# Nine pages of a first projection multiplied in high and low halves, with a norm and a clearing moved, in a two-block kernel on one Trainium2 core

## What is computed

```
h = rms_norm(x, norm1_g)
proj = h @ w_in
p_rwkv, p_sb, q_mem, gate_logits = split(proj)
y_a = rwkv7_branch(p_rwkv)          # token shift, low-rank paths, recurrence over 8 heads of 64
y_b = stick_breaking_branch(p_sb)   # q, k, v of 512 columns each
y_m = memory_branch(q_mem, mem)     # mem normed with mem_norm_g, then projected
x   = x + (sum of gated branches) @ w_out
x   = x + conv_ffn(x)
```

## Time and profile before

| | |
|---|---|
| runs | 1413.20, 1414.07, 1414.85 us |
| profiled execution, its span | 1414.9 us |
| PE busy | 1281.9 us (91%) |
| DVE, ACT, POOL busy | 835.0, 626.0, 585.6 us |
| chain that ended last | PE 59%, DMA 28%, DVE 6%, ACT 5% |
| mean granted TensorE clock | 0.988 |

### The profile page before, as it was taken

How to read it: one execution, slowest core, us unless ns; L and a number is a source line. 1 busy time by engine, 2 the same in 40 slices (tenths; PEclk the granted TensorE clock), 3 DMA queues, 4 the chain that set the end, 5 groups by cost and what they waited for, 6 DMA issues and landing times.

```text
span 1414.9 us, 22174 instructions
## 1 busy us (share of the span) xinstructions
PE 1281.9 (91%) x8684; PEld 904.4 (64%) x8684; DVE 835.0 (59%) x1897; ACT 626.0 (44%) x1449; POOL 585.6 (41%) x390
## 2 busy tenths in 40 slices
PE   7999999999999999999999999999778878777786
PEld 5887897888999999987897544444222323222222
DVE  3865210445557873477347676667776666677744
ACT  3310232556566665553454444444443444444433
POOL 1100022414878888740043544444434443343341
PEclk9999999999999999999999999999999999999999
DMA  6332321333545556542368999999999999999995
GB/s 240 105 120 92 105 93 60 120 105 134 195 164 186 181 186 194 165 134 98 137 232 340 421 421 421 422 421 422 421 422 421 421 418 422 422 422 422 422 422 226
DMA packets 67652, 381.06 MB, mean 269 GB/s; under 512 B 7520, under 2 KB 7648, under 8 KB 34528
## 3 DMA queue, kind: packets, MB, share of 16 engines
q0 software_dynamic: 36864, 268.45, 45.7%
q1 hardware_dynamic: 29808, 107.49, 22.5%
q10 hardware_dynamic: 880, 3.76, 0.7%
HBM read 378.63 MB, written 1.05 MB: 268 GB/s over the span
## 4 chain that ended last, share of the span: by engine, by line
PE 59%; DMA 28%; DVE 6%; ACT 5%; issue 2%; POOL 1%; DVEq 0%; POOLq 0%; ACTq 0%
DMA arena_block<-in_experts,arena_block 26%; PE bank L429 24%; PE bank L1023 10%; PE bank L465 4%; PE bank L983 3%; PE bank L483 3%; DVE arena_block L2218 2%; PE bank L427 2%; PE bank L447 2%; PE bank L853 1%; PE bank L516 1%; ACT arena_block L1517 1%; PE bank L542 1%; ACT arena_block L1515 1%; POOL w_lo L2276 1%
## 5 line engine op out<-in xcount | busy, mean ns | idle before, releaser
L1023 PE MATMUL bank<-arena_block 128*128 128x512 f32 x1024 | 494.8, 618 | 102.3 <-ACT arena_block L1517 102.3
L1023 PEld LDWEIGHTS bank<-arena_block 128*128 128x128 f32 x1024 | 183.1, 192 | 402.0 <-ACT arena_block L1517 246.0
L2218 DVE SCALAR_TENSOR_TENSOR arena_block<-arena_block 128x1024 f32<-128x1024 f32 x256 | 313.6, 1225 | 200.0 <-DMA arena_block<-in_experts,arena_block 199.4
L2292 POOL DMA_INDIRECT arena_block<-in_experts,arena_block x256 | 273.4, 1068 | 379.7 <-PE bank L1023 345.8
L2276 POOL TENSOR_TENSOR w_lo<-ring,w_hi 128x1024 fp32r<-128x1024 f32 x108 | 262.2, 2448 | 184.4 <-ACT w_hi L1083 184.1
L1511 ACT ACTIVATE arena_block<-arena_block 128x1 f32<-128x1 f32 x256 | 51.8, 202 | 322.2 <-DVE arena_block L2218 321.8
L1083 ACT ACTIVATE w_hi<-ring 128x1024 fp32r<-128x1024 f32 x116 | 122.0, 1053 | 60.1 <-PE bank L465 28.8
L429 PE MATMUL bank<-arena_mix,ring 128*128 128x256 f32 x480 | 110.8, 387 | 2.1 <-DMA const<-in_const 2.1
L429 PE MATMUL bank<-x_hi,w_hi 128*128 128x256 f32 x384 | 109.2, 284 | 1.6 <-POOL w_lo L2276 1.5
L429 PE MATMUL bank<-x_lo,w_hi 128*128 128x256 f32 x384 | 108.7, 283 | 0.0
L429 PE MATMUL bank<-x_hi,w_lo 128*128 128x256 f32 x384 | 108.7, 283 | 0.0
(11 more groups left out here) (503 smaller groups left out, 2247.0 us busy)
## 6 DMA issues: line engine op xcount, KB each, us to landing
ring<-in_pages SPq DMA_DIRECT2D x189, 512.0 KB, 3.8
late<-in_pages SPq DMA_DIRECT2D x11, 512.0 KB, 6.1
arena_block<-in_experts,arena_block POOLq DMA_INDIRECT x256, 15.3
x_res<-in_xT SPq DMA_DIRECT2D x2, 512.0 KB, 5.3
arena_mix<-in_memT ACTq DMA_DIRECT2D x1, 1024.0 KB, 10.1
arena_block<-in_subkT ACTq DMA_DIRECT2D x1, 1024.0 KB, 5.0
out_tok<-arena_block SPq DMA_DIRECT2D x4, 256.0 KB, 4.7
const<-in_const ACTq DMA_DIRECT2D x1, 974.5 KB, 7.4
```

The source lines that it names most:

```text
L1023: last = mm(bank[2 * tt + j][:, :], diag[:, slot, :], uv[slot][:, D + j * 512:D + (j + 1) * 512], start=False, stop=stop)
L2218: stt(uv[s][:, 0:D], uv[s][:, 0:D], 1.0, htok[:, tt, :], ALU.mult, ALU.mult, accum_out=e_act[:, s:s + 1])\
L2292: nc.gpsimd.indirect_dma_start(out=uv[slot], out_offset=None, in_=A["experts"], in_offset=bass.IndirectOffsetOnAxis(ap=eidx[:, tt, m:m + 1 ...
```

## The change

Pages 17 to 25 become split pages. Their high halves go in turn to three rooms in the arena (`first_hi`), their low halves stay in place in the ring. The input is split too: ACT writes `xg_hi` (eight activations behind the gate copies), DVE writes `xg_lo` (eight scalar_tensor_tensor behind `evict(11)`), which lies in two slots of `w_hi`. PE waits for both halves of the input once, ahead of page 17. The memset of `DT` and `norm_apply(1)` move behind `evict(25)` on DVE. A high half waits until the page three before it has been multiplied.

```
+FIRSTS = list(range(PAGE0["in_a"] + 17, PAGE0["in_a"] + N_IN_A))
+IN_PLACE = FIRSTS + EARLY
+SPLIT = IN_PLACE + [p for p in range(SPLIT0, N_PAGES) if p not in WHOLE]
...
+    first_hi = [typed(start, f"first_hi{i}", 4).rearrange("p a b -> p (a b)") for i, start in enumerate((8704, 13824, 14848))]
+    xg_hi = typed(9728, "xg_hi", KT)
+    xg_lo = w_hi[:, 0:2, :].rearrange("p s (k t) -> p (s k) t", t=T)
...
-            if page in EARLY:
-                high, low = early_hi[(page - EARLY[0]) % SLOTS], ring_lo[:, slot, :]
+            if page in IN_PLACE:
+                high, low = high_room(page), ring_lo[:, slot, :]
                 return [(high, hi), (high, lo), (low, hi)]
...
         def a_page(first, n=1):
-            linear("in_a", xg, part=(first, n))
+            if first == 17:
+                pe.wait_ge(S("xg_split"), KT)
+            if first < 17:
+                linear("in_a", xg, part=(first, n))
+            else:
+                linear("in_a", xg_hi, xg_lo, part=(first, n))
...
-            act.wait_ge(S("page_done"), page - 3)
+            act.wait_ge(S("page_done"), page - 2 if page in FIRSTS else page - 3)
+            A_(high_room(page), ring[:, page % SLOTS, :], ACT.Copy).then_inc(S("hi_ready"), 1)
...
         A_(gT[:, 2:4, :], two(bank[5][:, :], T), ACT.Copy).then_inc(S("b_act"), 1)
+        for k in range(KT):
+            A_(xg_hi[:, k, :], x[:, k, :], ACT.Identity, scale=V("norm1_g", k)).then_inc(S("xg_high"), 1)
...
         norm_root(1)
+        high(FIRSTS[0])
+        high(FIRSTS[1])
...
+        high(FIRSTS[2])
         act.wait_ge(S("b_pe"), B_PE["bktok"])
         A_(Btok, bank[6][:, :], ACT.Copy)
         A_(Ktok, bank[7][:, :], ACT.Copy).then_inc(S("b_act"), 1)
+        high(FIRSTS[3])
...
         last.then_inc(S("b_act"), 1)
+        high(FIRSTS[4])
         for lv in range(4):
...
             A_(PPn, two(bank[6][:, :], NEAR), ACT.Copy).then_inc(S("b_act"), 1)
+            if lv == 0:
+                high(FIRSTS[5])
+                high(FIRSTS[6])
+                high(FIRSTS[7])
+            if lv == 1:
+                high(FIRSTS[8])
...
-        v.memset(DT, 0.0)
         dve.wait_ge(S("b_act"), B_ACT["lora_taken"])
...
         evict(11, True)
+        for k in range(KT):
+            dve.wait_ge(S("xg_high"), k + 1)
+            stt(xg_lo[:, k, :], x[:, k, :], V("norm1_g", k), xg_hi[:, k, :].bitcast(F32), ALU.mult, ALU.subtract).then_inc(S("xg_split"), 1)
...
         evict(23)
-        norm_apply(1, mem_raw, "mem_g", memn)
         pairs_read(4)
...
         evict(25)
+        v.memset(DT, 0.0)
+        norm_apply(1, mem_raw, "mem_g", memn)
         near_cross(3)
```

More of the change, by code:

```diff
@@ L44 @@
 EARLY = list(range(PAGE0["gate0"], PAGE0["gate0"] + 16))
-SPLIT = EARLY + [p for p in range(SPLIT0, N_PAGES) if p not in WHOLE]
+FIRSTS = list(range(PAGE0["in_a"] + 17, PAGE0["in_a"] + N_IN_A))
+IN_PLACE = FIRSTS + EARLY
+SPLIT = IN_PLACE + [p for p in range(SPLIT0, N_PAGES) if p not in WHOLE]
 NTH = {p: i + 1 for i, p in enumerate(SPLIT)}
@@ L267, in build, with high_room @@
     x_hi, x_lo = (sb(n, [P, KT, T], F32R) for n in ("x_hi", "x_lo"))
+    xg_lo = w_hi[:, 0:2, :].rearrange("p s (k t) -> p (s k) t", t=T)
+    def high_room(page):
+        if page in FIRSTS:
+            return first_hi[(page - FIRSTS[0]) % 3]
+        if page in EARLY:
+            return early_hi[(page - EARLY[0]) % SLOTS]
+        return w_hi[:, page % SLOTS, :]
     ff_space = [nc.sbuf_tensor(n, [P, FT, T], F32R) for n in ("ff_hi", "ff_lo")]
@@ L363, in _ @@
         for page in range(SLOTS, LATE0 - 1):
-            if page - SLOTS in NTH and page - SLOTS not in EARLY:
+            if page - SLOTS in NTH and page - SLOTS not in IN_PLACE:
                 sp.wait_ge(S("lo_ready"), NTH[page - SLOTS])
@@ L1079, in high @@
             act.wait_ge(S(f"page_in{page % SLOTS}"), 16 * (page // SLOTS + 1))
-            act.wait_ge(S("page_done"), page - 3)
-            w = early_hi[(page - EARLY[0]) % SLOTS] if page in EARLY else w_hi[:, page % SLOTS, :]
-            A_(w, ring[:, page % SLOTS, :], ACT.Copy).then_inc(S("hi_ready"), 1)
+            act.wait_ge(S("page_done"), page - 2 if page in FIRSTS else page - 3)
+            A_(high_room(page), ring[:, page % SLOTS, :], ACT.Copy).then_inc(S("hi_ready"), 1)
         def high_ahead(page):
@@ L2271, in low @@
             pool.wait_ge(S("hi_ready"), n + 1)
-            if SPLIT[n] in EARLY:
-                high = early_hi[(SPLIT[n] - EARLY[0]) % SLOTS].bitcast(F32)
-                nc.gpsimd.tensor_tensor(ring_lo[:, slot, :], ring[:, slot, :], high, ALU.subtract).then_inc(S("lo_ready"), 1)
+            if SPLIT[n] in IN_PLACE:
+                nc.gpsimd.tensor_tensor(ring_lo[:, slot, :], ring[:, slot, :], high_room(SPLIT[n]).bitcast(F32), ALU.subtract).then_inc(S("lo_ready"), 1)
                 return
```

## The result

The changed kernel takes **1420.56 us** in the median (1418.85 to 1423.8, four runs), beside 1413.63 us for the kernel before in the same session. The ratio is 1.005, with a 95% interval from 1.0038 to 1.0062: 7 us slower, 5.4 to 8.8. The prediction was 1417.6 us with a range up to 1419.8. So the direction was right and the size too small by 3 us. The profiled execution of the changed kernel took 1420.88 us, its span 1418.8.

What follows compares the result with a forecast made beforehand. The prediction took PE as the bound, with the tightest wait on DVE at `pairs(1)`. Pages -5.5, stall +7.1, clock +1.7 and `pairs(7)` +0.2 gave +3.5 us on 1414.07, so 1417.6 us, range 1409.0 to 1419.8.

Steps and rivals of the forecast that it cites:

- The pages: Pages 17 to 25 on PE: nine split pages take 27.2 us instead of 32.65, saving 5.5 us (5.1 to 5.8).
- The stall: At `pairs(1)`: PE waits 7.1 us for `pairs_read(0)`, as `norm_apply(0)` on DVE takes turns with four POOL low halves.
- The clock behind it: Behind the wait at `pairs(1)`: part of the stretch at 1.2 GHz, 1.7 us, with 0 and twice it as bounds.
- `pairs(7)`: Behind page 25: PE waits 0.2 us more, as DVE has the memset and `norm_apply(1)` before reading `pairs(6)`.
- the first one: Between 100 and 120 us: PE, busy for 20.00 of 20.00 us at full clock, is the bound.
- The base: Start of the sum: 1414.07 us; the profiled span of 1414.9 was said to lie 0.8 above the runs' median.
- That the saving stays: Rival 1, at `norm_apply(0)`: DVE is hardly held up, PE waits 0.7 us at `pairs(1)`, 1409.5 us; chance 0.18.
- The longer stall: Rival 3: page 20's low half comes ahead of `near_ready`'s last step, `near_pp(0)` late; 1420 to 1422 us; chance 0.08.
- The shorter one: Rival 2: low halves fall out of POOL's train, 2.2 us each; 1415.4 us with one, 1413.2 with two; chance 0.14.
- The Trainium skill's pace for a single gap: Split pages on PE: 109 ns for 256 columns gives 2.6 us a page, 1415.6 us in all; the sum used the rows.
- The Trainium skill's rule of the exclusive lock: GpSimd and a two-SBUF-input DVE instruction lock a shared port for the whole instruction; without it the sum would be 1408.8 us.

Runs made afterwards that it cites:

- late apply: Changed kernel with `norm_apply(0)` moved behind `evict(23)`, where POOL has no low half to do: 1413.33 us, ratio to before 0.9997.
- The two runs that take away one of its two parties: Changed kernel with `norm_apply(0)` behind `evict(23)`, 1413.33 us; changed kernel without POOL's low halves of pages 20 to 23, 1411.84 us.
- the second profile: Changed kernel, unchanged, profiled a second time: 1425.55 us.
- the kernel with wide matmuls, 16 wide ones: Changed kernel with 16 matmuls of two columns ahead of PE's wait for the constants: 1421.54 us, ratio 1.0056.
- where the moves are alone: Kernel before with only the clearing of `DT` and `norm_apply(1)` moved behind `evict(25)`, no page split: 1413.86 us, ratio 0.9996.
- the second profiles: Both kernels profiled again without edit: kernel before 1414.44 us, changed kernel 1425.55 us.
- 16 small matmuls: Changed kernel with `norm_apply(0)` behind `evict(23)`, plus 16 matmuls of 32 rows and columns ahead of the constants: 2.4 us faster than the kernel before.
- 48 small: Changed kernel with `norm_apply(0)` behind `evict(23)`, plus 48 matmuls of 32 rows and columns ahead of the constants: 4.2 us above that without them.
- 32 small ones: Changed kernel with `norm_apply(0)` behind `evict(23)`, plus 32 matmuls of 32 rows and columns ahead of the constants: 1.1 us above that without them.

## Why the prediction was right, and where it failed

- **The pages** were forecast at -5.5 us, 0.61 each. A split page takes 3.06 us, and the period from one `pairs` to the next is 5.35 us in late apply where nothing comes between, against 5.93 before. That is 0.58 each, 5.2 us. Right but for 0.3.
- **The stall** was forecast at 7.1 us at `pairs(1)`, with the mechanism and the place. It is 6.6. The two runs that take away one of its two parties show the mechanism. The turns came as drawn: one instruction of 1.70 us and three of 2.56 to 2.62, where the prediction had 1.75 and three times 2.6. `norm_apply(0)` is held up by 7.56 us and not 7.95, which is nearly all of the half microsecond.
- **The clock behind it** was forecast at 1.7 us. The 5.7 us from `pairs(1)` to the next near product are 1.6 more than the usual 4.1. In the second profile and in the kernel with wide matmuls the low clock reached on into the stretch of 115 to 120 us (0.70 and 0.73), and the same way takes 6.61 and 6.65 us. So it is 1.6 to 2.5 us.
- **`pairs(7)`**, 0.2 us: 0.36 where the moves are alone, nothing in the changed kernel.
- **The missing term** is PE's idle at issue: 0.26 + 0.92 + 2.12 = 3.3 us, against 0.39 in the profile of before. The step that failed is the first one, which took PE as busy "for 20.00 of 20.00 us" and so as the bound, and asked only about waits for other engines. It did not ask what limits PE's own supply of instructions. The work of the change was priced by the time of the page, and the 16 instructions that each split page adds were counted at nothing.
- The sum with the measured terms: -5.2 + 6.6 + 1.6 + 2.9 = +5.9 us, and the first profiles of the two kernels differ by 5.9 from the product ahead of page 16 on. For the second profiles the terms are -5.2 + 6.6 + 2.5 + 3.3 + 1.6 = +8.8, the last for a stretch of lower clock behind the idle of 2.43 us; they differ by 8.7. The medians differ by 6.9, between the two. So the clock's term differs from one execution to the next, and the rest of the miss is the idle at issue.
- **The base** of the sum was stated loosely. I compared the span with the median of the times and found 0.8 us between them, but times are spans plus 2 us. The sum was added to the median, so the forecast was not shifted by it.
- **The rivals.** That the saving stays was ruled out by the 10.81 us. The longer stall, at 1420 to 1422, gives the right time for the wrong reason: the stall was, if anything, shorter. The shorter one did not come either: all four low halves were in the train.

The Trainium skill's pace for a single gap (TensorE: Matmul & The Clock Gate, Back-to-back issue gap), 2.6 us for a split page, did not come: 3.06 us. That formula is for a matmul by itself, as the page says, and a page of weights is a stream. The Trainium skill's rule of the exclusive lock (SBUF — State Buffer, Who interferes with whom) is borne out: 10.81 us with POOL's low halves beside it, 3.25 without.

## What to carry to other kernels

When work is put on an engine that shares something with another, look for the place where the other has a train of instructions of the sharing kind, and move one of the two: here one line moved by four evicts was worth 7 us. Count instructions as well as time: where PE got through 256 of them in less than some 3.3 us, its supply was the bound, and a change elsewhere in the program that adds a few can move a stall of 2 us in or out. A small difference between two versions of such a kernel may be nothing but that, so shift the stream by a few instructions before a change of 2 or 3 us is believed, and read from the trace what these take themselves. And before small matmuls are spread among large ones, count the changes, at 0.28 to 0.30 us here for one there and back.

## What the runs showed of the hardware that I had not expected

- PE's instruction blocks: 16.4 KB each, one for 256 instructions, never less than 3.25 us apart, no more than one ahead of PE as far as these stalls show. A packet takes 0.9 us, and up to 2.0 us; PE goes on 1.2 to 1.6 us after its end.
- 128 matmul records of 32 by 32 take 1.2 us, 9.5 ns each, in a near product, but 32 ns each where all are of the same 32 rows. A change from matmuls of 128 rows to these and back costs 0.28 us.
- PE's idle time alone does not say whether its clock falls. Before 15 us an idle of 1.1 to 1.6 us left the clock of the next 5 us at 1.00 in four profiles and one of 2.1 to 2.5 us brought it to 0.66 in five. But with 16 small matmuls ahead of it an idle of 1.21 us brought it to 0.66 too, and so did 48 small or 16 wide ones without any idle, while 32 small ones left it at 1.00. And at 150 to 160 us idle times of 2.12, 2.13 and 2.45 us left it full, and behind another of 2.43 us and one of 2.82 us it fell. Stretches at the lower level of 1.2 GHz, worth some 1.7 us each, also come where PE was busy throughout: both profiles of the change and both of late apply have one between 255 and 275 us, at about the same matmuls, and neither profile of before has; of the other versions only that with 16 small matmuls has it. What brings them is open. The twelve runs of late apply differ by 7.3 us (1410.3 to 1417.6), more than four such stretches; why they do is open too.
